# Interleaving the mLSTM inner stage with the last gate blocks of its up projection

## What is computed

```python
xm, z = jnp.split(u @ w_up, 2, axis=-1)
xc = jax.nn.silu(conv_centred(xm, conv_w, conv_b))
q, k, v = blockdiag(xc, w_q), blockdiag(xc, w_k), blockdiag(xm, w_v)
gates = jnp.concatenate([q, k, v], axis=-1) @ w_gate + b_gate
...
# per head and direction; in chunks of 64 here, all tokens at once in the kernel
dmat = jnp.where(mask, b[..., :, None] - b[..., None, :] + ic[..., None, :], -jnp.inf)
s = jnp.einsum('bhjd,bhsd->bhjs', qc, kc) * jnp.exp(dmat - m_j[..., None])
h = num / jnp.maximum(jnp.abs(qn), jnp.exp(-m_j))[..., None]
...
h = h_fwd + h_bwd          # normalised over each head's 512 channels
h = (h + skip * xc) * jax.nn.silu(z)
y_lat = h[:, n_ctx:] @ w_down
```

## Time and profile before

| | |
|---|---|
| median of 3 runs | 2040.59 us (2035.99 to 2043.72) |
| profiled execution | 2036.21 us |
| its span | 2034.5 us |
| mean granted clock of PE | 0.983 |
| PE busy | 1964.9 us (97%) |
| DVE busy | 1227.5 us (60%) |
| ACT busy | 638.0 us (31%) |
| POOL busy | 86.1 us (4%) |

### The profile page before, as it was taken

The page is one execution under the profiler, slowest core; times in us unless marked ns, Lnnn a source line. Parts: engine busy times, 40 slices in busy tenths (PEclk is TensorE's granted clock), DMA queues, the critical chain, the costliest instruction groups (busy, mean ns, idle before and its releaser), DMA issues.

```text
span 2034.5 us, 25023 instructions
## 1 busy us (share of the span) xinstructions
PE 1964.9 (97%) x9588; PEld 1582.1 (78%) x9588; DVE 1227.5 (60%) x1615; ACT 638.0 (31%) x656; POOL 86.1 (4%) x157
## 2 busy tenths in 40 slices
PE   8899999999989999999999999999999997899999
PEld 3588888877867778888888788888867776599998
DVE  5876766568568666776755866232373356764445
ACT  4522222233231132222223322122243353444343
POOL 0011000000000000100000000000000002000000
PEclk9899999999999999999999999999999997999999
DMA  9255555422220015555542455222312123044552
GB/s 344 96 197 206 183 189 186 144 83 83 103 98 1 33 63 186 196 193 189 196 141 97 146 188 183 103 86 100 134 63 78 57 83 134 1 145 165 186 179 110
DMA packets 48320, 272.02 MB, mean 134 GB/s; under 512 B 5380, under 2 KB 6020, under 8 KB 24840
## 3 DMA queue, kind: packets, MB, share of 16 engines
q1 hardware_dynamic: 28536, 194.69, 27.0%
q0 software_dynamic: 19728, 76.55, 11.0%
HBM read 270.18 MB, written 1.05 MB: 133 GB/s over the span
## 4 chain that ended last, share of the span: by engine, by line
PE 89%; DVE 8%; ACT 2%; issue 1%; DMA 0%; POOL 0%; DVEq 0%; SPq 0%; ACTq 0%
PE ps L1381 26%; PE ps L1383 25%; PE ps L1382 25%; PE ps L1662 2%; PE ps L1374 2%; DVE tn L864 2%; PE ps L1742 1%; DVE act_lo L850 1%; PE ps L1821 1%; PE ps L1652 1%; DVE w_lo L774 1%; PE ps L1705 1%; ACT w_hi L400 1%; PE ps L1567 1%; ACT act_hi L428 0%
## 5 line engine op out<-in xcount | busy, mean ns | idle before, releaser
L1381 PE MATMUL ps<-act_hi,w_hi 128*128 128x512 f32 (+1 forms) x2728 | 986.6, 362 | 19.5 <-DVE w_lo L774 10.2
L1382 PE MATMUL ps<-act_lo,w_hi 128*128 128x512 f32 (+1 forms) x2728 | 981.1, 360 | 0.0
L1383 PE MATMUL ps<-act_hi,w_lo 128*128 128x512 f32 (+1 forms) x2728 | 981.0, 360 | 0.0
L774 DVE TENSOR_TENSOR w_lo<-w_raw,w_hi 128x2048 fp32r<-128x2048 f32 x172 | 394.1, 2291 | 492.5 <-ACT w_hi L400 492.5
L1381 PEld LDWEIGHTS ps<-act_hi,w_hi 128*128 128x128 f32 x2728 | 517.8, 190 | 106.9 <-DVE w_lo L774 11.6
L1383 PEld LDWEIGHTS ps<-act_hi,w_lo 128*128 128x128 f32 x2728 | 517.8, 190 | 76.0
L1382 PEld LDWEIGHTS ps<-act_lo,w_hi 128*128 128x128 f32 x2728 | 517.8, 190 | 75.6 <-issue 0.5
L400 ACT ACTIVATE w_hi<-w_raw 128x2048 fp32r<-128x2048 f32 x172 | 329.2, 1914 | 629.3 <-PE ps L1383 629.3
L790 DVE SCALAR_TENSOR_TENSOR ada_w<-ada_w,cond_bc 128x1024 f32<-128x1024 f32 x128 | 156.3, 1221 | 0.0
L790 DVE SCALAR_TENSOR_TENSOR ada_prod<-ada_w,cond_bc 128x1024 f32<-128x1024 f32 x128 | 156.2, 1220 | 0.0
L440 ACT ACTIVATE silu_g<-ps 128x1024 f32<-128x1024 f32 (+1 forms) x44 | 40.5, 920 | 307.3 <-PE ps L1383 307.2
(11 more groups left out here) (212 smaller groups left out, 1081.6 us busy)
## 6 DMA issues: line engine op xcount, KB each, us to landing
w_raw<-w_stream_dram SPq DMA_DIRECT2D x172, 1024.0 KB, 4.8
ada_w<-ada_rows_dram POOLq DMA_DIRECT2D x128, 512.0 KB, 3.6
ada_raw<-ada_stream_dram POOLq DMA_DIRECT2D x4, 1024.0 KB, 11.8
...
```

Of the source, the lines that this page charges most:

```text
L774: dve.tensor_tensor(w_lo[:, g % 2, :], w_raw[:, g % 2, :], w_hi[:, g % 2, :].bitcast(F32), ALU.subtract).then_inc(w_lo_done, 1)
L1381: pe.matmul(out, wh, xh, start=start, stop=False)
L1382: pe.matmul(out, wh, xl, start=False, stop=False)
L1383: return pe.matmul(out, wl, xh, start=False, stop=stop)
```

## The change

- **z blocks.** Each z block from 1 on writes one PSUM bank, 2 or 3 by turns, its two tiles one after the other (before, the tiles alternated within each of the 8 steps of the contraction). The loop is written out. PE's order is now: gate spread, z1, z2, z3, `spread(0)`, z4, the column turn, z5, `turn_p(0)`, `spread(1)`, z6, `turn_p(1)`, sum 0, z7, and then `turn_p(it)` and sum `it` - 1 by turns. z1 moves behind the gate spread.
- **Gate spread.** Its rows go to banks 6 and 7 first, which do not wait for the last score copy.
- **Masks.** POOL masks a head as soon as its scores are copied. Only the 128 columns on the diagonal are multiplied; the rest is copied or zeroed. The second direction goes to the context half of `h`, which the last layer no longer needs. The mask is 128x2x128, loaded before block 115 into space of `row_g`'s second half, so that `row_g` now waits for `masked` 16.
- **Buffers.** `pd` of even iterations, `pt`, `acols` and `ht` move: to the space of `row_i`/`row_f`, to `cond_pad`, and to the context halves of `act_hi` and `act_lo`. `pc` and `score_b` are gone: the combined matrix is written over `pd`.
- **Spreads.** All heads use banks 4 and 5, so `spread(hd)` waits for all Exp of the heads before it.
- **Splits.** DVE's low halves: block 126 (of z3) moves from ahead of the gate rows to behind the log forget gate; 129 stays ahead of the iterations; 130, 131 and 132 go behind iterations 0, 1 and 2. ACT's high halves follow the z blocks as before, so their Silu now stands between the Exp of the iterations.

```diff
-        mask = over("mask", [P, 2, 2, LAT], act_at)
-
-        pd = [over("pd0", [P, 2, TOK], act_at + 4096), over("pd1", [P, 2, TOK], ada_at + 4096)]
+        mask = over("mask", [P, 2, P], ada_at + 14336)
+
+        pd = [over("pd0", [P, 2, TOK], tmp_at), over("pd1", [P, 2, TOK], ada_at + 4096)]
         w_comb = over("w_comb", [P, IT, 2, 16], tmp_at + 4160)
-        score_b = over("score_b", [P, HEADS, 2, LAT], tmp_at)
-        ht = [over(f"ht{j}", [P, INNER], act_at + 8192 + 16384 * j) for j in range(2)]
-        pt = over("pt", [P, 2, 4, P], act_at + 16384)
-        pc = over("pc", [P, TOK], act_at + 20480)
-        acols = over("acols", [P, 256], act_at + 22528)
+        ht = [over(f"ht{j}", [P, KT, TOK], act_at + 16384 * j)[:, :, 0:CTX] for j in range(2)]
+        pt = over("pt", [P, 2, 4, P], tmp_at + 4096)
+        acols = cond_pad[:].rearrange("p k c -> p (k c)")
...
+            sp.dma_start(mask[:], dram["mask"]).then_inc(s_mask, 16)
...
-            sp.wait_ge(w_used, G_MLDN)
-            sp.dma_start(mask[:], dram["mask"]).then_inc(s_mask, 16)
...
-            pool.wait_ge(row_dve, ROW["g"])
             for it in range(8):
                 hd, jt = it // 2, it % 2
+                now, rest = slice(CTX + jt * P, CTX + jt * P + P), slice(CTX + P, TOK)
                 pool.wait_ge(sc_evac, hd + 1)
-                pool.tensor_tensor(score_b[:, hd, jt], score[:, hd, jt, LATC], mask[:, 1, jt], ALU.mult).then_inc(masked, 1)
+                if jt == 0:
+                    pool.tensor_copy(h[:, it, P:CTX], score[:, hd, jt, rest])
+                else:
+                    pool.memset(h[:, it, 0:P], 0.0)
+                pool.tensor_tensor(h[:, it, jt * P:jt * P + P], score[:, hd, jt, now], mask[:, 1],
+                                   ALU.mult).then_inc(masked, 1)
                 pool.wait_ge(masked, 2 * it + 1)
-                pool.tensor_tensor(score[:, hd, jt, LATC], score[:, hd, jt, LATC], mask[:, 0, jt],
-                                   ALU.mult).then_inc(masked, 1)
+                if jt == 0:
+                    pool.memset(score[:, hd, jt, rest], 0.0)
+                pool.tensor_tensor(score[:, hd, jt, now], score[:, hd, jt, now], mask[:, 0], ALU.mult).then_inc(masked, 1)
...
-            def z_step(j, i=0, split=True):
-                act.wait_ge(w_used, G_MLUP + 9 + j + 2 * i)
-                act.activation(zs[:, bass.ds(2 * j + 4 * i, 2), :], ps[:, 2 * (j % 2):2 * (j % 2) + 2, LATC],
-                               ACT.Silu).then_inc(z_evac, 1)
+            def z_step(z, split=True):
+
+                act.wait_ge(w_used, G_MLUP + 9 + z)
+                src = ps[:, 0:2, LATC] if z == 0 else ps[:, 2 + z % 2, :].rearrange("p (t n) -> p t n", t=2)
+                act.activation(zs[:, 2 * z:2 * z + 2, :], src, ACT.Silu).then_inc(z_evac, 1)
                 if split:
-                    split_w(G_MLUP + 10 + j, i)
+                    split_w(G_MLUP + 10 + z)
...
             z_step(0, split=False)
-            z_step(1)
             act.wait_ge(row_dve, ROW["abs"])
             act.activation(row_c[R], row_c[R], ACT.Exp, scale=-1.0).then_inc(row_act, 1)
             act.wait_ge(row_act, 1)
             act.activation(row_c[R], row_c[R], ACT.Ln, bias=col("one")[R]).then_inc(row_act, 1)
+            z_step(1)
             z_step(2)
             z_step(3)
             act.wait_ge(row_dve, ROW["m"])
             act.activation(row_c[R], row_d[R], ACT.Exp, scale=-1.0).then_inc(row_act, 1)
             z_step(4)
-            z_step(5)
-            z_step(6)
-            z_step(7, split=False)
...
-                    act.wait_ge(a_dve, A_STEPS * (it - 1))
+                    act.wait_ge(pt_done, it - 1)
...
-                    act.activation(pd[it % 2][:, dr, :], ps[:, 4 - 2 * (hd % 2) + dr, :], ACT.Exp,
+                    act.activation(pd[it % 2][:, dr, :], ps[:, 4 + dr, :], ACT.Exp,
                                    bias=acols[:, c:c + 1]).then_inc(a_exp, 1)
...
+            def turned(it):
+
                 act.wait_ge(pt_done, it + 1)
                 if it >= 2:
                     act.wait_ge(pv_done, it - 1)
                 act.activation(pt[:, it % 2], ps[:, 6 - 5 * (it % 2), :].rearrange("p (a c) -> p a c", a=4),
                                ACT.Copy).then_inc(pt_evac, 1)
-                if it == 0:
-                    split_w(G_MLUP + 17)
-                if it == 6:
-                    deviation(0)
+
+            weights(0)
+            weights(1)
+            z_step(5)
+            turned(0)
+            weights(2)
+            z_step(6)
+            turned(1)
+            weights(3)
+            values(0)
+            z_step(7)
+            turned(2)
+            for it in range(4, 8):
+                weights(it)
+                values(it - 3)
+                turned(it - 1)
+            deviation(0)
+            values(5)
+            turned(7)
             normalize(0)
...
-            split_w(G_MLUP + 11)
...
+            split_w(G_MLUP + 11)
             scans(row_d, row_f, None, ALU.add, ("cum0", "cum1", "cum2", "cum3"))
             dve.wait_ge(row_dve, ROW["cum3"])
+            dve.wait_ge(masked, 16)
             dve.tensor_tensor(row_g[R], row_i[R], row_d[R], ALU.subtract).then_inc(row_dve, 1)
             split_w(G_MLUP + 12)
             scans(row_e, row_g, True, ALU.max, ("max0", "max1", "max2", "max3"))
             dve.wait_ge(row_dve, ROW["max3"])
             dve.tensor_tensor(row_d[R], row_d[R], row_e[R], ALU.add).then_inc(row_dve, 1)
-            for g in range(G_MLUP + 13, G_MLUP + 17):
-                split_w(g)
+            split_w(G_MLUP + 13)
+            split_w(G_MLUP + 14)
...
-                if it > 0:
-                    dve.wait_ge(pt_done, it)
-                dve.tensor_scalar(pc[:], p[:, 0, :], rd[:, 0:1], None, ALU.mult).then_inc(a_dve, 1)
+                dve.tensor_scalar(p[:, 0, :], p[:, 0, :], rd[:, 0:1], None, ALU.mult).then_inc(a_dve, 1)
                 dve.wait_ge(a_dve, n + 8)
-                dve.scalar_tensor_tensor(pc[:], p[:, 1, :], rd[:, 1:2], pc[:], ALU.mult, ALU.add).then_inc(a_dve, 1)
-                if it == 1:
-                    split_w(G_MLUP + 17)
+                dve.scalar_tensor_tensor(p[:, 0, :], p[:, 1, :], rd[:, 1:2], p[:, 0, :], ALU.mult, ALU.add).then_inc(a_dve, 1)
+                if it < 3:
+                    split_w(G_MLUP + 15 + it)
...
-            up(9)
-
             pe.wait_ge(row_dve, ROW["gsum1"])
             pe.wait_ge(gates_out, 2)
-            pe.wait_ge(sc_evac, HEADS)
             pe.wait_ge(v_evac, IT)
-            for r in range(4):
+            for r in (2, 3, 0, 1):
+                if r == 0:
+                    pe.wait_ge(sc_evac, HEADS)
                 mm = pe.matmul(ps[R, 4 + r, :], col("gate_sel", 4 * r, 4), gsum[:], start=True, stop=True)
             mm.then_inc(sel_done, 1)
 
-            def z_block(j, i):
-                pe.wait_ge(z_evac, j - 1 + 2 * i)
-                in_block(G_MLUP + 8 + j, i, 2 * (j % 2), LATC)
-
-            with pe.Fori(0, 3) as i:
-                z_block(2, i)
-                z_block(3, i)
+            def z_block(z):
+
+                g = G_MLUP + 8 + z
+                pe.wait_ge(w_lo_done, g + 1)
+                if z == 1:
+                    pe.wait_ge(xm_ready, 16)
+                elif z > 2:
+                    pe.wait_ge(z_evac, z - 1)
+                wh = w_hi[:, g % 2, :].rearrange("p (k c) -> p k c", c=256)
+                wl = w_lo[:, g % 2, :].rearrange("p (k c) -> p k c", c=256)
+                for t in range(2):
+                    c = slice(t * P, t * P + P)
+                    for k in range(KT):
+                        mm = product(ps[:, 2 + z % 2, t * LAT:t * LAT + LAT], (wh[:, k, c], wl[:, k, c]),
+                                     (act_hi[:, k, LATC], act_lo[:, k, LATC]), k == 0, k == KT - 1)
+                mm.then_inc(w_used, 1)
+
             def spread(hd):
 
-                if hd >= 2:
-                    pe.wait_ge(a_exp, 4 * (hd - 1))
+                if hd:
+                    pe.wait_ge(a_exp, 4 * hd)
+                else:
+                    pe.wait_ge(row_dve, ROW["g"])
                 for dr in range(2):
-                    mm = pe.matmul(ps[:, 4 - 2 * (hd % 2) + dr, :], ident[R, hd:hd + 1].to_broadcast([HEADS, P]),
+                    mm = pe.matmul(ps[:, 4 + dr, :], ident[R, hd:hd + 1].to_broadcast([HEADS, P]),
                                    row_g[R, dr, :], start=True, stop=True)
                 mm.then_inc(bc_done, 1)
 
-
+            z_block(1)
+            z_block(2)
+            z_block(3)
+            spread(0)
+            z_block(4)
...
+            z_block(5)
+            turn_p(0)
+            spread(1)
+            z_block(6)
+            turn_p(1)
+            weighted(0)
+            z_block(7)
+            for it in range(2, 8):
+                turn_p(it)
+                if it in (2, 4):
+                    spread(it // 2 + 1)
+                weighted(it - 1)
```

(5 more changed lines are left out.)

33 lines of the change are left out of this document (9 added, 24 removed).

## The result

| | before | changed |
|---|---|---|
| median (6 runs each) | 2041.84 us | 2025.62 us |
| lowest, highest | 2034.33, 2043.89 | 2024.30, 2027.08 |
| profiled execution, its span | 2036.21, 2034.5 | 2026.71, 2024.7 |
| mean granted clock of PE | 0.983 | 0.986 |

The ratio is 0.993, with a 95% interval of 0.9918 to 0.9942: 11.8 to 16.7 us of 2041.84. The medians lie 16.2 us apart, the profiled executions 9.5. The forecast was 2026.7, and 13.9 us less.

The account below looks back on a forecast made before the run. PE bounds the kernel; only its waits and lower clock can be won. Work 86.2 plus waits 1.8, 2.7, 2.9, 1.2 gives 94.8 against 112.1; less 3.4 for clock, 13.9 gained: 2040.6 to 2026.7 us, range 2020 to 2034.

Parts of the forecast that it names:

- z3's gap of 1.8: Ahead of z3, PE waits 1.8 us for a low half, as z1's Silu is queued behind the gate rows.
- `turn_p(0)`, 2.7: Ahead of `turn_p(0)`, PE idles 2.7 us until iteration 0 ends, behind z4's Silu, a table load and the first Exp.
- `turn_p(3)`, 2.9: Ahead of `turn_p(3)`, PE waits 2.9 us, as iteration 3 stands behind block 132's low half, which hangs on z7's end.
- PE's own work, 86.2: From 1652.8 to the last sum's end, PE's work at full clock was put at 86.2 of 112.1 us.
- The clock, 2 x 1.7: Behind the gaps of 2.7 and 2.9, a lower PE clock was charged 1.7 us each, 3.4 in all.
- Tail, costed at nothing: Behind the last sum, the tail with its wait of 3.26 us keeps its order and costs nothing more.
- Table loads at nothing: Six further ACT loads, 7.7 us, stand where ACT would wait for z blocks; only one, ahead of iteration 0, counted.
- POOL beside the gate rows at nothing: POOL's masks beside DVE's gate rows cost nothing, since those rows read PSUM or 4 partitions; 2.4 us kept for the range.
- that no clock is lost: Rival, 15%: no gap of PE pulls its clock down, so 17.3 us less, 2023.3 us.
- DVE slowed by POOL: Rival, 17%: POOL slows the gate rows by 2.4 us, z3's gap becomes 4.2; 9.8 us less, 2030.8.
- ACT as the bound: Rival, 6%: a table switch holds ACT for twice its load, so 7.1 us less, 2033.5 us.
- The clock that stays down: Rival, 5%: PE's clock, low at `turn_p(0)`, stays low through the 51.5 us of work from there; slower, 2070.7 us.

Follow-up runs that it names:

- experiments 6 to 10: Changed kernel with PE's waits filled by matmuls (128, then 32 columns), then three reorders of splits and weights: 2022.94, 2022.04, 2024.36, 2021.31, 2020.13 us.
- experiment 10: Changed kernel with first two weights ahead of z4's Silu, splits 129 to 132 behind iterations 0 to 3, block 126 split between Exp and Ln: 2020.13 us.
- 8: Changed kernel with DVE's split of block 132 behind iteration 3 instead of iteration 2: 2024.36 us, 0.9916 of the kernel before.
- 9: Changed kernel with ACT's first two weights ahead of z4's step and DVE's splits of 129 to 132 behind iterations 0 to 3: 2021.31 us.
- kernels filled to size: Changed kernel with 8, 8 and 13 unused matmuls ahead of z3, `turn_p(0)` and `turn_p(3)`, 128 or 32 columns: 2022.94 and 2022.04 us.
- 2: Changed kernel with z blocks 5 to 7 emptied by Copy instead of Silu, six table loads fewer: 2025.57 us, 0.9925 of the kernel before.
- 3: Changed kernel with a square root ahead of each Silu of z blocks 5 to 7, adding table loads: 2025.85 us, 0.9932 of the kernel before.
- 4: Changed kernel with each of POOL's second-direction mask products made five times: 2023.83 us, 0.9919 of the kernel before.

## Why the prediction was right

Step by step, on its own walk:

- **What bounds the kernel**: right. With the waits of PE filled to size or removed, and nothing else, the stretch gets shorter (experiments 6 to 10), and in experiment 10 the time falls clear of noise.
- **z3's gap of 1.8**: 1.93. The gate rows set it, as said: Exp, load, Ln, load, Silu followed each other without a gap from 1664.02 to 1668.85.
- **`turn_p(0)`, 2.7**: 1.98. **`turn_p(3)`, 2.9**: 3.04. The cause of `turn_p(3)`'s is the one named, since moving that one split removed it (8). `turn_p(0)`'s went with ACT's weights and DVE's splits moved together (9), which fits the cause named and does not single it out. z4 to z7 waited for nothing. The short waits came to 1.1 against 1.2.
- **PE's own work, 86.2**: 1.2 too little. The gate spread starts 6.96 behind the start of the last score product (1656.39 - 1649.43) where z1 had started 6.46 behind it, and a z block behind other work took 5.94 (1673.63 to 1679.57) instead of 5.76, five times or so.
- **The clock, 2 x 1.7**: the term that was mis-sized. The two gaps cost up to 3.4 and 1.7, together 5.1, since the first was followed by 6.8 us at 1.2 GHz and not 3.4; by the kernels filled to size it was 4.5. That a gap of 1.8 costs nothing held here.
- **Sum**: the walk had 98.2 for what took 118.6 - 6.5 = 112.1 before; measured 100.6 (11.5 less). The 2.4 between them are 1.7 of clock, 1.2 of work, and 0.5 of waits the other way (with 4.5 for the clock, 1.1 and 1.8). The stretch gave 11.5 instead of 13.9. The interval of the whole kernel, 11.8 to 16.7, holds the forecast; the 11.5 lie just below it.
- **Luck in the number**: 2025.62 is 1.1 from the forecast because errors met. The stretch gave 2.4 less than the walk, while the medians differ by some 5 us more than the stretch, 1.4 of them in the tail and the others, by the granted clocks given above, in low periods that no trace here shows. For the profiled execution the walk gives 2022.3, and it took 2026.71. The mechanism was right; that the time came so close is partly luck.
- **Tail, costed at nothing**: its wait was, 3.25 against 3.26; the period at the lower clock behind it comes and goes (it is there in seven of the eleven experiments). This term should have had a range of 0 to 1.7, and so should the place near 468 us.
- **Table loads at nothing**: right, in both directions (2, 3). **POOL beside the gate rows at nothing**: right (4). In the xm blocks both engines paid a little: beside DVE's conv steps a product of POOL took 1.00 instead of 0.45, and steps of DVE took 0.84 and 0.68 where the kernel before had 0.75 and 0.54. All six steps of a head took 0.3 to 0.5 us longer, with 15.13 us of idle time ahead of them; the bound had been 3.9.
- **Rivals**: that no clock is lost did not come true for this kernel, but for the two that were filled to size, 102.6. DVE slowed by POOL, and ACT as the bound, were refuted by their own experiments. The clock that stays down did not occur: no period in the stretch of the changed kernel and its variants was longer than 6.8 us, against 20.5 in the trace of before and 10.2 with the early masks alone.
